# A decoder layer on one core: the last attention stage taken by pairs of units, with its row sums from a column of ones

## The reference, cut to what matters

```python
scs = jnp.einsum('bqgrd,bqgkd->bqgrk', qb, kg).astype(jnp.float32) * scale
scs = scs - slopes[None, None, :, :, None] * dist.astype(jnp.float32)
p = jax.nn.softmax(jnp.where(dist >= 0, scs, NEG), axis=-1)
return jnp.einsum('bqgrk,bqgkd->bqgrd', p.astype(vg.dtype), vg)
...
o_win = banded_attention(q, kw, vw, C_WINDOW, slopes)
return gates[..., 0:1] * o_cmp + gates[..., 1:2] * o_slc + gates[..., 2:3] * o_win
```

## Time and profile before

| | us |
|---|---|
| median of 3 runs | 773.97 |
| lowest, highest | 770.73, 774.15 |
| the profiled execution, its own time | 772.57 |
| its span (first to last instruction) | 770.6 |
| the stage of the change, first exp to the last output (475.9 to 668.8) | 192.9 |
| one head in it, from the third on | 23.15 |

### The profile page before, as it was taken

One profiled execution on the slowest core, in us unless ns is written; L12 is line 12 of the kernel. 1 busy time (PEld: TensorE's weight loads), 2 busy tenths in 40 slices (PEclk: granted clock), 3 DMA queues, 4 the chain that ended last, 5 costly groups with the idle time before them and its releaser, 6 DMA issues.

```text
span 770.6 us, 15601 instructions
## 1 busy us (share of the span) xinstructions
PE 726.2 (94%) x5980; PEld 625.1 (81%) x5980; DVE 543.6 (71%) x1263; ACT 420.8 (55%) x982; POOL 189.7 (25%) x118
## 2 busy tenths in 40 slices
PE   4999999999999999889999998989999999899996
PEld 4999878687777777668888886978999999788885
DVE  4796222044888888967779997998999999934232
ACT  5774122013566656657733333878999999722211
POOL 2674000000000000000143343416276552122120
PEclk9999999999999999999999999999999999999999
DMA  8620548165135621143154323300003101143331
GB/s 330 204 82 27 195 133 230 51 186 166 54 90 134 171 81 56 55 127 108 56 135 117 111 69 89 80 2 2 2 3 111 57 3 57 64 155 119 129 109 55
DMA packets 34090, 77.13 MB, mean 100 GB/s; under 512 B 5472, under 2 KB 14048, under 8 KB 33376
## 3 DMA queue, kind: packets, MB, share of 16 engines
q1 hardware_dynamic: 34016, 76.13, 32.6%
HBM read 57.77 MB, written 18.35 MB: 99 GB/s over the span
## 4 chain that ended last, share of the span: by engine, by line
PE 58%; DVE 15%; ACT 14%; issue 8%; DMA 4%; POOL 1%; SPq 1%; ACTq 0%; DVEq 0%; POOLq 0%
ACT n_probs L1783 5%; ACT n_probsT_high L1793 4%; DVE n_probs L1846 4%; PE o_acc L2224 3%; PE o_acc L2223 3%; PE o_acc L2222 3%; PE a_projected L199 3%; PE a_projected L201 3%; PE a_projected L200 3%; PE nat L823 3%; PE s_projected L199 3%; PE features L809 2%; PE s_projected L201 2%; PE s_projected L200 2%; PE n_turned L865 2%
## 5 line engine op out<-in xcount | busy, mean ns | idle before, releaser
L1783 ACT ACTIVATE n_probs<-n_probs,n_negated_max 128x640 f32<-128x640 f32 (+7 forms) x128 | 94.9, 741 | 18.3 <-DVE n_negated_max L1846 17.4
L1855 DVE SCALAR_TENSOR_TENSOR n_probsT_low<-n_turned,n_probsT_high 128x512 f16<-128x512 f32 (+3 forms) x192 | 94.4, 520 | 14.3 <-ACT n_probsT_high L1793 11.8
L183 POOL TENSOR_TENSOR w_and_keys_low<-w_raw,w_and_keys_high 128x1024 fp32r<-128x1024 f32 x6 | 15.0, 2503 | 290.6 <-ACT w_and_keys_high L168 290.4
L865 PE MATMUL n_turned<-identity,n_probs 128*128 128x128 f32 x528 | 81.8, 280 | 3.5 <-ACT n_probs L1783 2.8
L1793 ACT ACTIVATE n_probsT_high<-n_turned 128x512 f16<-128x512 f32 (+3 forms) x192 | 81.0, 457 | 4.6 <-PE n_turned L865 4.0
L1994 PE MATMUL n_scores<-w_and_keys_high,stacks 128*128 128x256 f32 (+2 forms) x192 | 74.4, 388 | 4.4 <-DVE n_negated_max L1846 4.3
L865 PEld LDWEIGHTS n_turned<-identity,n_probs 128*128 128x128 f32 x528 | 61.5, 143 | 12.4 <-ACT n_probs L1783 9.2
L1995 PE MATMUL n_scores<-w_and_keys_low,stacks 128*128 128x256 f32 (+2 forms) x192 | 61.6, 332 | 0.0
L199 PE MATMUL a_projected<-xT_high,w_and_keys_high 128*128 128x512 f32 x144 | 57.4, 398 | 0.9 <-ACT staged L208 0.7
L201 PE MATMUL a_projected<-xT_high,w_and_keys_low 128*128 128x512 f32 x144 | 56.4, 392 | 0.0
L200 PE MATMUL a_projected<-xT_low,w_and_keys_high 128*128 128x512 f32 x144 | 56.4, 391 | 0.0
(11 more groups left out here) (289 smaller groups left out, 2142.0 us busy)
## 6 DMA issues: line engine op xcount, KB each, us to landing
w_raw<-in_w_feat SPq DMA_DIRECT2D x23, 512.0 KB, 4.0
weights_then_b_and_s_raw<-features SPq DMA_DIRECT2D x30, 256.0 KB, 4.7
stacks<-a_parts SPq DMA_DIRECT2D x48, 128.0 KB, 3.9
features<-staged SPq DMA_DIRECT2D x22, 256.0 KB, 4.3
branches_b_c<-in_x SPq DMA_DIRECT2D x8, 512.0 KB, 4.3
silu_gates<-staged SPq DMA_DIRECT2D x16, 256.0 KB, 2.0
gatesT<-silu_gates SPq DMA_DIRECT2D x8, 512.0 KB, 5.5
keys_and_w_out_raw<-in_w_out SPq DMA_DIRECT2D x4, 1024.0 KB, 5.1
```

What stands on the lines that cost most here:

```text
L865: mm = nc.tensor.transpose(dst[:, j, :], src[:, c:c + P], ident[:, :])
L1783: nc.scalar.activation(pr[:, n % PS, 0:w], pr[:, n % PS, 0:w], ACT.Exp, scale=-1.0, bias=nmax[:, hb % 4, qt:qt + 1], accum_out=sums[:, hb ...
L1855: nc.vector.scalar_tensor_tensor(out=ptl[:, g % GS, 0:k, :], in0=tp[g % TS][:, 0:k, :], scalar=PSCALE, in1=pth[:, g % GS, 0:k, :], op0=ALU ...
```

## The change

The change does four things in the last attention stage.

1. The loops of PE, ACT and DVE go by pairs of a wide and a narrow unit. PE does both scores, then both turns, then both values. DVE does both biases, then both low parts. ACT does high_part(n) and then exponentials(n+2), for each of the two.
2. The row sums no longer come from ScalarE's accumulator (except in the last block). The high values get a 65th column of ones, so that the output carries the sum beside the 64 values. The tiles `values_b_and_selected` and `values_window` grow from 64 to 66 fp16 a head and part; two memsets at the start write the ones. The reciprocal reads the 65th column of `n_out`. The sums then carry the factor 2^14 too, and the gates of the two branches get it as a factor.
3. Output bank 0 takes the wide units and bank 1 the narrow ones, in every block. ACT brings a block out in two copies of 260 columns after exp(n+2) of the next block's first pair: it waits for the values of the block's last wide unit, and of its last narrow one. PE waits for these copies (`n_out_copied`) before the next block's first write into each bank.
4. `invert_sums` comes after the low part of a block's fourth unit (was second), waits for the copies, and POOL no longer waits for `headed`, which only the last block raises now.

```diff
@@ values_run @@
-def values_run(nc, out, ph, pl, run, v_of_tile, opens, closes, parts=2):
+def values_run(nc, out, ph, pl, run, v_of_tile, opens, closes, parts=2, sums=False):
+    widths = [HV if sums and part == 0 else HD for part in range(parts)]
     for j, kt in enumerate(run):
         v = v_of_tile(kt)
-        for part in range(parts):
-            nc.tensor.matmul(out, ph[:, j, :], v[:, part, :], start=(opens and j == 0 and part == 0), stop=False)
-        for part in range(parts - 1):
-            mm = nc.tensor.matmul(out, pl[:, j, :], v[:, part, :], start=False,
+        for part, w in enumerate(widths):
+            nc.tensor.matmul(out[:, 0:w], ph[:, j, :], v[:, part, 0:w], start=(opens and j == 0 and part == 0), stop=False)
+        for part, w in enumerate(widths[:-1]):
+            mm = nc.tensor.matmul(out[:, 0:w], pl[:, j, :], v[:, part, 0:w], start=False,
                                   stop=(closes and j == len(run) - 1 and part == parts - 2))
@@ start_phase, vector @@
+            nc.vector.memset(vbs[:, :, :, 0, HD:HV], 1.0)
+            nc.vector.memset(vw[:, :, :, 0, HD:HV], 1.0)
@@ cmp_phase, vector @@
-                                                vscale[:, 1, br:br + 1], None, ALU.mult))
+                                                vscale[:, 1, br:br + 1], PSCALE, ALU.mult, ALU.mult))
@@ nsa_phase, scalar @@
-                nc.scalar.activation(pr[:, n % PS, 0:w], pr[:, n % PS, 0:w], ACT.Exp, scale=-1.0,
-                                     bias=nmax[:, hb % 4, qt:qt + 1], accum_out=sums[:, hb % 4, qt:qt + 1]).then_inc(exped, 1)
+                x, least = pr[:, n % PS, 0:w], nmax[:, hb % 4, qt:qt + 1]
+                if hb == LAST:
+                    ins = nc.scalar.activation(x, x, ACT.Exp, scale=-1.0, bias=least, accum_out=sums[:, hb % 4, qt:qt + 1])
+                else:
+                    ins = nc.scalar.activation(x, x, ACT.Exp, scale=-1.0, bias=least)
+                ins.then_inc(exped, 1)
...
             def bring_out(hb):
-                act.wait_ge(valued, before[NT * (hb + 1)])
+                act.wait_ge(valued, before[NT * (hb + 1) - 1])
...
-                nc.scalar.copy(red[:, hb % 2, :, :], ov[hb % 2][:, :].rearrange("p (q d) -> p q d", q=NT)).then_inc(headed, 1)
+                nc.scalar.copy(red[:, hb % 2, NT // 2:NT, :], ov[0][:, :, :]).then_inc(copied, 1)
+                act.wait_ge(valued, before[NT * (hb + 1)])
+                nc.scalar.copy(red[:, hb % 2, 0:NT // 2, :], ov[1][:, :, :]).then_inc(copied, 1)
             exponentials(0)
-            for n in range(UN):
-                if n + 1 < UN:
-                    exponentials(n + 1)
-                high_part(n)
-                if n % NT == 2 and n > NT:
-                    bring_out(n // NT - 1)
+            exponentials(1)
+            for wide in range(0, UN, 2):
+                for n in (wide, wide + 1):
+                    high_part(n)
+                    if n + AHEAD < UN:
+                        exponentials(n + AHEAD)
+                    if n == wide and n % NT == 0 and n > 0:
+                        bring_out(n // NT - 1)
@@ nsa_phase, vector @@
-                dve.wait_ge(exped, NT * (hb + 1))
-                nc.vector.reciprocal(s, s).then_inc(inverted, 1)
+                if hb == LAST:
+                    dve.wait_ge(exped, NT * (hb + 1))
+                    ch.link(nc.vector.tensor_scalar(s, s, PSCALE, None, ALU.mult))
+                    nc.vector.reciprocal(s, s).then_inc(inverted, 1)
+                else:
+                    dve.wait_ge(copied, 2 * (hb + 1))
+                    nc.vector.reciprocal(s.unsqueeze(2), red[:, hb % 2, :, HD:HV]).then_inc(inverted, 1)
...
-            for n in range(UN):
-                if n + AHEAD < UN:
-                    add_bias(n + AHEAD)
-                low_part(n)
...
-                if n % NT == 1 and n > NT:
-                    invert_sums(n // NT - 1)
+            for wide in range(0, UN, 2):
+                pair = (wide, wide + 1)
+                for n in pair:
+                    if n + AHEAD < UN:
+                        add_bias(n + AHEAD)
+                for n in pair:
+                    low_part(n)
...
+                    if n % NT == 3 and n > NT:
+                        invert_sums(n // NT - 1)
@@ nsa_phase, tensor @@
-                if n % NT == 0 and hb >= 2:
-                    pe.wait_ge(headed, hb - 1)
+                if n % NT < 2 and hb >= 1:
+                    pe.wait_ge(copied, 2 * hb - 1 + n % NT)
...
-                    values_run(nc, ov[hb % 2][:, HD * qt:HD * (qt + 1)], pth[:, g % GS], ptl[:, g % GS], run,
+                    values_run(nc, ov[n % 2][:, qt % (NT // 2), :], pth[:, g % GS], ptl[:, g % GS], run,
...
-            for n in range(UN):
-                if n + AHEAD < UN:
-                    scores(n + AHEAD)
-                turn(n)
-                if n >= 2:
-                    values(n - 2)
+            for wide in range(0, UN, 2):
+                pair = (wide, wide + 1)
+                for n in pair:
+                    if n + AHEAD < UN:
+                        scores(n + AHEAD)
+                for n in pair:
+                    turn(n)
+                for n in pair:
+                    if n >= 2:
+                        values(n - 2)
```

40 lines of the change are left out of this document (21 added, 19 removed).

## The result

| | before | after |
|---|---|---|
| median, us | 774.06 (4 runs, 770.73 to 775.03) | 780.63 (4 runs, 778.83 to 780.93) |
| profiled execution, its span | 772.57, 770.6 | 778.83, 777.0 |
| one head, third on | 23.15 | 23.89 |

The ratio is 1.0097, with an interval from 1.0074 to 1.0120: slower by about 1%, where 768 us and "faster" were forecast, and outside the range of 761 to 776. Of the 6.4 us of span, the third to seventh heads give 3.5 (four of them 0.74 each, the third 0.6). The stage starts 1.2 us later, the first two heads together are 0.25 shorter, and from the eighth head's first bias to the end it takes 129.9 us in place of 128.0 (127.95).

The account below looks back on a forecast made before the run. PE's work and the DVE-ACT loop, both 22.1 to 22.2 us a head, were taken to bound jointly. PE 21.7, loop 22.1 and 0.3 friction gave 22.4 a head, 5.8 us saved: 768 us, range 761 to 776.

Parts of the forecast that it names:

- The copies: ACT, two copies of 260 columns inside the loop: 0.52 us a block, 1.04 a head, giving the read's gain back.
- The sum: PE 21.7 and loop 22.1 us give a head of 22.4; 8 heads save 6.0, less 0.2: 5.8 us.
- friction: Time of a head beyond PE's work and the loop, as either is late: 1.0 us before, 0.3 expected after.
- The prediction's loop: DVE and ACT: wide bias, wide exp, narrow high part, narrow low part, next wide bias; 22.1 us a head before and after.
- scores in pairs: PE, a second score group behind the first changes operands cheaply: 0.54 us a head saved, bounds 0 to 0.86.
- 65th column: PE, two of three value matmuls get one column more: 0.0005 us each, 132 times a head, 0.06 us.
- The end: After the last values: one more linked instruction, 0.2 us, and weighing about 0.1 longer, partly hidden; +0.2 us in all.
- Rival 3: Block boundary: ACT waits at its second copy for values, up to 1.1 us, 15 times; 785 us; chance 0.09.
- Rival 1: DVE and ACT's loop takes back the gain, friction near the old one: a head 23.0, 773 us; chance 0.25.
- Rival 4: PE, the odd width of 65 columns is slow: at twice the time about 799 us; chance 0.04.
- Rival 2: Friction vanishes and a head runs at PE's own 21.7 us: 762.6 us; chance 0.17.
- The reading of the case: Kernel before: PE's work and the DVE-ACT loop both 22.1 to 22.2 us of a 23.15 us head; neither alone bounds.

Follow-up runs that it names:

- e1: The changed kernel with ScalarE's two copies of a finished block behind the pair's second exp, not the first; 771.02 us, ratio 0.9976.
- e2: The changed kernel with the 64 value columns left out of both copies from the third block on, same place; 772.77 us, ratio 1.0010.
- e11: The changed kernel with each of a block's two copies made twice at the same place; 787.04 us (one run).
- e4: The changed kernel with the old unit-by-unit order on PE, DVE and ACT, copies behind the second unit's high part; 770.68 us, ratio 0.9974.
- e3: The kernel before with the order by pairs alone, its one copy behind the pair's second exp; 773.09 us, ratio 1.0001.
- e12: e1 with both high parts of a pair ahead of both exps on ScalarE; 772.24 us, ratio 1.0005.
- e7: The changed kernel with PE's values of each unit directly behind its turn, DVE and ACT still in pairs; 773.89 us, ratio 1.0017.
- e6: The kernel before with PE alone in pairs: scores, scores, turn, values, turn, values; 791.19 us, ratio 1.0225.

## Why the prediction was wrong

**The step that failed** is "The copies" together with "The sum": it added the copies' 1.04 us to a round averaged over the head's eight pairs, set that against the read's gain, and put 0.3 us of friction on the larger sum. The length was right (0.53 measured, 0.52 forecast). The averaging was not. The copies fall into two pairs of eight, next to the widest narrow unit, and what PE loses there it doesn't get back in the other six. e1, e2 and e11 show it: the copies cost their full length, on PE, at every boundary. The timeline shows what was late: the narrow unit's low part, which frees the bank, and some 0.2 us ahead of it the next narrow unit's exp. The prediction's loop runs over the wide exp alone and has no place for the narrow one, which stands behind copies and high part too. Why PE can't make it up is argued and not shown: the three banks `n_turned` hold just one pair (two chunks and one), and PE turns the next pair only when its exps are there. The lower bound of that step, "0 if ACT is ahead at that place", and the expectation of "one hand-over each way a pair in place of two" both pointed the wrong way. A pair order has fewer hand-overs and also nothing between them to do.

**Term by term**, for a head:

| term | forecast | measured |
|---|---|---|
| scores in pairs, on PE | −0.54 (0 to −0.86) | −0.68 to −0.77 (8.60, against 9.28 in the forecast's sum and 9.37 in e4) |
| 65th column | +0.06 | +0.27 (5.76 to 6.03) |
| PE's own work after | 21.7 | 21.83 (7.2 + 6.03 + 8.60) |
| no read, per exp | 0.09 and 0.04 | 0.11 (603.07 to 603.79 is 0.72, was 0.83 with the read) |
| two copies | 0.52 a boundary | 0.53 |
| head beyond PE's own work | 0.7 (22.4 − 21.7: 0.4 to the loop's 22.1, friction 0.3) | 2.06, nearly all in T (9.24 − 7.2) |
| head | 22.4 | 23.89 |

The span was to fall by 5.8 us and grew by 6.4. Of these 12.2 us 10.3 are in the eight heads, and 1.9 stand outside them (start and end of the stage, below). Of a head's error, 1.5 us, PE's own work is 0.13 and the wait beyond it 1.36: 1.04 of the 2.06 goes with the copies' place (T of after less T of e1), and the 1.0 left is what the pair order itself costs (T of e1 above 7.2). e3 has the pair order without the sums; there the scores' gain is turned into the same kind of wait. The copies' part is shown three ways. That the rest is the round of DVE and ACT in the pair with the widest narrow unit is borne out by e12, which moved it but did not remove it. A fourth bank `n_turned` was not tried. In the order of the changed kernel it could give back only some 0.2 us a boundary, by the rows above (an estimate): the exp of the same tiles is ready only 0.22 to 0.23 us before the bank, with the copies in the middle, last (e1: 600.18 and 600.40) or made twice (e11: 610.92 and 611.14).

**The 65th column** was priced by the neighbour with 64 columns at 0.0005 us a matmul; it costs 0.27 us a head. V reads 6.02 to 6.06 in the kernels that have the column (6.90 in e7, with a wait in it) and 5.76 or 5.77 in before and e3 (5.86 in e6). It is too small to turn the sign. The starts of single matmuls say where it lies. Each key tile has three: high part with 65 columns, high part with 64, low part with 65. From the first to the second it is 29.3 ns in the changed kernel (mean of 528; before 29.2), and from the third to the next tile's first 29.2 (464; before 29.6). From the second to the third it is 33.3 (528), and 29.5 before. So the matmuls with 65 columns keep the spacing of 64, and the 0.27 us are 66 times the 4 ns that the step from the 64-column matmul to the low part's has gained. It stands in every kernel with the column of ones (33.3 to 33.7) and in none without; why it is this step was not tested. By the Trainium skill (TensorE: Matmul & The Clock Gate, Back-to-back issue gap) 65 columns would be 29.6 ns, an estimate; the 29.2 and 29.3 behind matmuls of 65 columns agree, and the 33.3 is not in it.

**The end** was put at +0.2. From the eighth head's first bias to the end the changed kernel takes 2.0 us more, e1 1.0, e4 0.8, e3 0.2. Of the 2.0, 1.0 is there when the last value matmul starts (26.16 us after that bias, before 25.13; e4 25.06), so it is the eighth head's own. The other 0.9 comes with the sums half and accrues in the output projection, whose code the change doesn't touch: from the first to the last matmul into `o_acc` it takes 93.1 us (e4 93.1) against 92.3 (e3 92.4). One of its three steps, from a matmul of `stacks` with `o_yT_high` to the next, takes 232 or 233 ns in the median in every kernel with the sums half, and 227 in those without. The weighing and the linked instruction, on which the forecast put its +0.2, are not where it lies. Which edit of that half does it, for one the wider value tiles, was not separated. The start of the stage, 1.2 us later, stands beside a fall of the clock at 438.7 us, outside the change's code, that the trace before does not have.

**The rivals.** Rival 3 was nearest in sign and in place (ACT at its copies, at the block boundary) and wrong in mechanism: it priced a wait of up to 1.1 us a boundary for the values, and at the copies ACT did not wait. The rule of the Trainium skill that spoke for it (Perfetto Trace Analysis, Optimizing Tensor Performance), on rotating output groups through banks, is not what decided: nothing waits for the output banks in the changed kernel's trace. What counted was the copies' own length. Rival 1 had the mechanism that was shown, a gain given back to the loop of DVE and ACT, but its bound of 23.0 a head came from the same averaging. Rival 4 was real and small, 0.27 us a head, but in the step behind the 64-column matmul and not at the odd width itself. Rival 2 is nearest to e4, in which PE never stands: friction vanished there, in unit order and not in pairs.

**The reading of the case** before the change, that neither PE nor the loop alone is the bound, held. It was used the wrong way: where two rounds are equal, an instruction put into one of them is not paid out of the slack of the other.

## What to carry to other kernels

Work out a round for the worst pair, not as a mean over pairs, and for every instruction that a turn needs (here the exp as well as the bank); whether more banks would let the slack of one pair carry to the next was not tried here. An instruction that nobody waits for yet goes behind the ones that the bound engine waits for, and its place can be worth its whole length each time (1.05 us a head here). When two engines' rounds are equal, a saving on one of them alone may give little or nothing (e3; 0.5 us in e4), and reordering can turn it into a wait elsewhere: sum the groups of the bound engine, as T, V and S here, to see whether a saving stays or moves.

## What the runs showed of the hardware

- Among short fp16 matmuls the start behind one of 65 columns comes after 29.2 to 29.3 ns, as behind one of 64 in the kernel before. The step from a high part's 64-column matmul to a low part's of 65 columns takes 33.3 ns, where it took 29.5 with 64 columns throughout.
- The same code of the output projection runs slower in every kernel with the column of ones: 232 ns in place of 227 for one step in three, 0.8 us over 384 matmuls. The cause is open.
- ScalarE's exp without the accumulator starts the next instruction 0.11 us earlier (0.83 to 0.72 for 640 columns), nearly all of it the read's own 0.09. A copy of four columns still takes about 0.06 us to the next start.
- The 3.4 us falls of the granted clock to 0.50 came at different places and in different number from kernel to kernel (two in the stage before, one of 6.8 us after), and shift a total by one or two us (the second head: 27.7 us with a fall, 25.7 without).
